# Weighing stage in the program of the expert-activation stage, with the first group prepared in freed buffers

## The chip, the cores and the metric

One core of one Trainium2 chip. The metric is the device time of one execution in microseconds; before the change three runs gave 3397.03, 3400.71 and 3400.64, median 3400.64.

## The reference

A transformer layer over 1024 tokens of width 1024. After the attention part, which the change doesn't touch, comes PEER: every token has 8 heads, each picks 16 of 16,384 single-neuron experts by product keys, and

```python
hid = jnp.einsum('td,tkd->tk', xx, u[ee])          # 128 picks a token
act = jax.nn.gelu(hid, approximate=False) * gg     # gg: softmax share of a pick
out = jnp.einsum('tk,tkd->td', act, v[ee])
```

## The kernel before

Tokens are cut into 8 blocks of 128. Blocks 0 and 1 (`GB = 2`, "first" tokens) are done by gathering the picked rows of `u` and `v`; blocks 2 to 7 (`TD = 768` tokens) densely over all experts, with a gate table that is zero where an expert isn't picked. All matmuls run as three passes of a high and a low fp32r part: high x high, high x low, low x high. A high part is a copy on ScalarE, a low part a subtraction on POOL (GpSimd).

`hidden` (L774) is the **expert-activation stage**: 8 blocks x 16 slots, one slot for each of 128 key rows j. A slot loads `u_raw` on the SyncE queue, rounds it (`u_hi`, ScalarE L918; `u_lo`, POOL L968), runs 48 matmuls of 384 columns (L1299), takes Gelu of them into `hid` (L943) and stores it to `hid_d`. From block 2 on a slot also makes the gate table of 8 tokens: one-hot factors on VectorE (L1017), scaling on ScalarE (L924), 8 matmuls (L1312), a copy to `stage` (L951) that SyncE stores to `gate_d` in quarters of half a block (64 tokens). Beside it, POOL gathers one row of `u` for each first token and pick (L977) and VectorE takes the dot product with `x_first` (L1228) into `pick_act`: `LAG = (8, 16)` slots after the start for the two blocks, and the last 8 and 16 picks in the last block into the freed score table (L987, L1235). Then Gelu and share.

`weigh` (L1788) is the **weighing stage**, in a program block of its own: the one before has to end on all engines first. It sums activation x gate x v over 32 groups of 4 key rows. A group has two halves of 2 rows. For a half SyncE loads `v_raw` (1 MB, one buffer) and `act_in` (768 KB, one buffer a half) and once a group `gate_in` (1.5 MB, one buffer); VectorE multiplies gates in (L1940), ScalarE rounds (`v_hi` L1897, `act_hi` L1899), POOL makes `v_lo` (L1924) and `act_lo` (L1929). TensorE then runs, for each of 6 token blocks, 24 matmuls of 512 columns (L2006; 144 a group) into one of two PSUM accumulators `part`, and VectorE adds that to `acc` (L1945). For the first tokens POOL gathers a row of `v` for each pick k (`found`, 4 buffers; two DMAs, L1915) and VectorE adds it to `first_sum` (L1953): 128 picks, four a group in all 32 groups.

The order on each engine is written out by hand, and every engine works strictly in its order. What matters here: a buffer's next load waits on SyncE until its low part is made; a gather waits on POOL until its buffer's last pick is summed, and the low parts stand behind it; on VectorE the product with the gates of the group after next stands between the adds:

```python
add(g, 4)
if left >= 2:
    gates(g + 2, 0)
add(g, 5)
add_pick(g, 3)
```

TensorE's wait for a group's halves stands at token block 0, ahead of row 0 and of row 2.

Of the kernel before, what the change touches and what calls it, by code (L numbers as in the profile page):

```python
# [396 lines left out]

class Shared:

    def __init__(self, nc, c, sem):  # L400
        self.banks = c.enter_context(nc.psum_tensor("banks", [P, 8, HALF], F))

        with ExitStack() as first:
            def sb(name, shape, dt=F):
                return first.enter_context(nc.sbuf_tensor(name, shape, dt))
# [23 lines left out]
        self.pick = sb("pick", [P, PEER_HEADS, K], U32)
        self.share = sb("share", [P, PEER_HEADS, K])  # L430
        self.col_t = sb("col_t", [P, P])
        self.score = sb("score", [P, 2 * PEER_HEADS, NK])
        self.found = sb("found", [P, GB, D])
        self.stage = sb("stage", [P, 2, NK, 64])
        self.top = sb("top", [P, PEER_HEADS, 2, K])
        self.top_ix = sb("top_ix", [P, PEER_HEADS, 2, K], U32)
        self.top_ixf = sb("top_ixf", [P, PEER_HEADS, 2, K])
        self.pick_part = sb("pick_part", [P, 2, PEER_HEADS, K], U32)
        self.expert = sb("expert", [P, 2, PEER_HEADS, K])
        self.row_t = sb("row_t", [P, P])  # L440
        self.g_t = sb("g_t", [P, P])
        self.pick_u = sb("pick_u", [P, GB, PICKS], U32)
        self.pick_share = sb("pick_share", [P, GB, PICKS])
# [6 lines left out]
        self.sc_out = sem("sc_out")  # L450


def route(nc, block, sem, m, a_hi, a_lo, x_first, ident, x_d, w_out_d, norm_g_d, wq_d, keysT_d, h_d, uT_d, score_d):
# [10 lines left out]
    with ExitStack() as c:  # L464
        def sb(name, shape, dt=F):
            return c.enter_context(nc.sbuf_tensor(name, shape, dt))

        w_raw, w_hi, w_lo, h, xs, gain, keysT = m.w_raw, m.w_hi, m.w_lo, m.h, m.xs, m.gain, m.keysT
        qT = xs[:, 0].rearrange("p (s n) -> p s n", s=2)
        rest = xs[:, 1, 0:HALF].rearrange("p (b n) -> p b n", b=4)  # L470
        sc = xs[:, 1, HALF:D].rearrange("p (b n) -> p b n", b=4)
        top, top_ix = m.key_top, m.key_ix
        tick = sb("tick3", [P, 4])
        ss = sb("ss3", [P, TB])
        rstd = sb("rstd3", [P, TB])
        neg_half = sb("neg_half3", [P, 1])
        pr_ps = m.banks[:, 0:4]
        tr_ps = m.banks[:, 4:6].rearrange("p b (c n) -> p (b c) n", c=C // 2)
        sc_ps = m.banks[:, 6:8].rearrange("p s (b n) -> p s b n", b=4)

        x_in = sem("x_in3")
        small_in = sem("small_in3")

        first_in = [sem(f"first_in3{n}") for n in range(4)]
        first_hi = sem("first_hi3")
        first_lo = [sem(f"first_lo3{n}") for n in range(4)]
        w_in = sem("w_in3")
        w_hi_ok = sem("w_hi_ok3")
        w_lo_ok = sem("w_lo_ok3")
        u_in, u_hi_ok, u_lo_ok = m.u_in, m.u_hi_ok, m.u_lo_ok  # L490
        const_ok = sem("const_ok3")
        pr_ok = sem("pr_ok3")
        added = sem("h_added")
        h_out = sem("h_out")
        ss_ok = sem("ss_ok3")
        var_ok = sem("var_ok3")
        rstd_ok = sem("rstd_ok3")
        xs_ok = sem("xs_ok3")
        tr_ok = sem("tr_ok3")
        hi_ok = sem("hi_ok3")  # L500
        lo_ok = sem("lo_ok3")
        q_ok = m.q_ok
        sc_ok = sem("sc_ok")
        first_ok = sem("first_ok3")
        rest_ok = sem("rest_ok3")
        second_ok = sem("second_ok3")
        top_ok = m.top_ok
        sc_sb = sem("sc_sb")
        sc_out = m.sc_out
        SCORED = 4 * ITEMS  # L510

        @block.sync
        def _(sp):
            def load_w(g):
                src = w_out_d[:, g * HALF:(g + 1) * HALF] if g < 2 else wq_d[:, (g - 2) * HALF:(g - 1) * HALF]
                if g == 1:
                    for part in range(4):
                        sp.wait_ge(first_lo[part], 1)
                else:
                    sp.wait_ge(w_lo_ok, 4 * (g - 1))  # L520
                sp.dma_start(w_raw[:, :, :], src.rearrange("(c p) n -> p c n", p=P)).then_inc(w_in, 16)

            def load_u(j):
                sp.dma_start(m.u_raw[:, :, :], uT_d[j]).then_inc(u_in, 16)

            for part in range(4):
                s = slice(2 * part, 2 * part + 2)
                sp.dma_start(w_raw[:, s], w_out_d[2 * part * P:(2 * part + 2) * P, 0:HALF]
                             .rearrange("(c p) n -> p c n", p=P)).then_inc(first_in[part], 16)
            sp.dma_start(h[:, :, :], x_d.rearrange("(b p) n -> p b n", p=P)).then_inc(x_in, 16)  # L530
            sp.dma_start(gain[:, :], norm_g_d.unsqueeze(0).to_broadcast([P, D])).then_inc(small_in, 16)
            load_w(1)
            sp.dma_start(keysT[:, :, :], keysT_d.rearrange("k d n -> d k n")).then_inc(small_in, 16)
            load_w(2)
            for tb in range(TB):
                sp.wait_ge(added, TB + tb + 1)
                sp.dma_start(h_d[tb * P:(tb + 1) * P, :], h[:, tb]).then_inc(h_out, 16)
            load_w(3)
            for n in range(SCORED):
                if n == ITEMS:  # L540
                    load_w(4)
                if n == 2 * ITEMS:
                    load_w(5)
                if n == 3 * ITEMS:
                    sp.wait_ge(xs_ok, TB)
                    load_u(0)
                if n == SCORED - 2:
                    sp.wait_ge(u_lo_ok, 1)
                    load_u(1)
                key = n // 2  # L550
                if n % 2:
                    sp.wait_ge(sc_sb, key + 1)
                    sp.dma_start(score_d[:, :, key * NK:(key + 1) * NK].rearrange("b t n -> t b n"),
                                 sc[:, :, :]).then_inc(sc_out, 16)

        @block.gpsimd
        def _(pool):
            pool.memset(neg_half[:, :], -0.5).then_inc(const_ok, 1)
            pool.wait_ge(const_ok, 1)

            def split_low(g):
                for part in range(4):
                    s = slice(2 * part, 2 * part + 2)
                    pool.wait_ge(w_hi_ok, g)
                    pool.tensor_tensor(w_lo[:, g % 2, s], w_raw[:, s], w_hi[:, g % 2, s].bitcast(F),
                                       ALU.subtract).then_inc(w_lo_ok, 1)

            for part in (0, 2):
                s = slice(2 * part, 2 * part + 2)
                pool.wait_ge(first_hi, part + 1)  # L570
                pool.tensor_tensor(w_lo[:, 0, s], w_raw[:, s], w_hi[:, 0, s].bitcast(F),
                                   ALU.subtract).then_inc(first_lo[part], 1)
            split_low(1)
            for tb in range(TB):
                pool.wait_ge(var_ok, tb + 1)
                pool.tensor_tensor(rstd[:, tb:tb + 1], ss[:, tb:tb + 1], neg_half[:, 0:1],
                                   ALU.pow).then_inc(rstd_ok, 1)
                if tb == 2:
                    split_low(2)
# [1552 lines left out]
```

## Time and profile before

| | us |
|---|---|
| median of 3 runs | 3400.64 |
| profiled execution | 3400.2 |
| its span, first to last instruction | 3398.4 |
| TensorE busy | 3167.1 |
| VectorE, POOL, ScalarE busy | 2187.0, 1693.5, 1222.5 |
| first matmul of `hidden` / of `weigh` | 1009.2 / 2317.4 |
| last matmul chain of `weigh` ends | 3381.5 |

The profile is one execution. Times are from the span's start. "PEclk" is the granted clock of TensorE as a share of 2.4 GHz, "<-" names what ended an idle time. A busy share over the whole span says little here; the rows below are therefore read by stretch.

### The profile page before, as it was taken

The page shows a single profiled execution, that of the slowest core. Times are in us where ns is not written, and L with a number is a line of the kernel's source. Part 1 is how long each engine was busy: PE and PEld are TensorE (multiplying, and loading weights), DVE is VectorE, ACT ScalarE, POOL GpSimd, SP SyncE. Part 2 cuts the span into 40 slices and gives each one's busy share as a digit, 9 for nine tenths or more (in the row PEclk, how much of TensorE's full clock was granted, in tenths as well). Part 3 has the DMA queues.
Part 4 walks back from the last instruction along what each step waited for, and adds up shares of the span by engine and source line. Part 5 has one row for each costly group of instructions (what it writes and reads, how often), then busy time and mean ns, then how long its engine had stood idle before and what let it go on. Part 6 is the DMA issues. An engine that isn't in the chain of part 4 may idle for free. (4 is left out here: it accounts for less than half of the span.)

```text
span 3398.4 us, 44061 instructions
## 1 busy us (share of the span) xinstructions
PE 3167.1 (93%) x17090; PEld 2861.5 (84%) x17090; DVE 2187.0 (64%) x3550; ACT 1222.5 (36%) x1895; POOL 1693.5 (50%) x847
## 2 busy tenths in 40 slices
PE   7989688988999999999999999985999999999998
PEld 5777578877889999999999999984888888888886
DVE  2510578824456778788988888763766666666665
ACT  3211347722112225656565656651122211222110
POOL 2411010012103565555556555765877878778683
PEclk9999799999999999999999999997999999999999
DMA  3242651141213676767677767898878778787784
GB/s 137 87 167 75 154 112 41 35 161 62 72 41 132 201 238 203 248 236 249 235 247 238 251 234 237 314 329 319 298 284 308 278 280 308 270 306 283 274 295 162
DMA packets 253394, 713.78 MB, mean 210 GB/s; under 512 B 21680, under 2 KB 79920, under 8 KB 246576
## 3 DMA queue, kind: packets, MB, share of 16 engines
q1 hardware_dynamic: 179504, 443.13, 38.2%
q0 software_dynamic: 73728, 268.47, 22.9%
q8 instruction: 104, 1.70, 0.2%
q14 instruction: 58, 0.48, 0.0%
HBM read 577.31 MB, written 134.22 MB: 209 GB/s over the span
## 5 line engine op out<-in xcount | busy, mean ns | idle before, releaser
L1228 DVE SCALAR_TENSOR_TENSOR found<-found,x_first 128x1024 f32<-128x1024 f32 x232 | 393.9, 1708 | 238.4 <-DMA found<-in_u,pick_u 237.5
L968 POOL TENSOR_TENSOR u_lo<-u_raw,u_hi 128x1024 fp32r<-128x1024 f32 x127 | 353.8, 2786 | 367.0 <-ACT u_hi L918 366.6
L1299 PE MATMUL banks<-side_hi,u_hi 128*128 128x384 f32 x2048 | 528.5, 339 | 0.0
L2006 PE MATMUL part<-v_hi,act_hi 128*128 128x512 f32 x1536 | 475.9, 391 | 48.9 <-POOL act_lo L1929 48.0
L1299 PE MATMUL banks<-side_hi,u_lo 128*128 128x384 f32 x2048 | 520.3, 334 | 0.0
L1299 PE MATMUL banks<-side_lo,u_hi 128*128 128x384 f32 x2048 | 520.2, 334 | 0.0
L2006 PE MATMUL part<-v_lo,act_hi 128*128 128x512 f32 x1536 | 474.8, 390 | 0.0
L2006 PE MATMUL part<-v_hi,act_lo 128*128 128x512 f32 x1536 | 474.6, 390 | 0.0
L977 POOL DMA_INDIRECT found<-in_u,pick_u x232 | 334.7, 1443 | 188.9 <-DVE found L1228 148.5
L1945 DVE TENSOR_TENSOR acc<-acc,part 128x1024 f32<-128x1024 f32 x192 | 234.1, 1219 | 297.6 <-PE part L2006 297.4
L1897 ACT ACTIVATE v_hi<-v_raw 128x2048 fp32r<-128x2048 f32 x64 | 122.8, 1919 | 808.9 <-DMA v_raw<-in_v 623.9
L1924 POOL TENSOR_TENSOR v_lo<-v_raw,v_hi 128x2048 fp32r<-128x2048 f32 x64 | 295.8, 4621 | 190.4 <-ACT v_hi L1897 189.8
L2006 PEld LDWEIGHTS part<-v_hi,act_hi 128*128 128x128 f32 x1536 | 289.5, 189 | 110.6 <-issue 49.0
L1299 PEld LDWEIGHTS banks<-side_hi,u_lo 128*128 128x128 f32 x2048 | 370.2, 188 | 0.0
L1299 PEld LDWEIGHTS banks<-side_lo,u_hi 128*128 128x128 f32 x2048 | 370.1, 188 | 0.0
L1299 PEld LDWEIGHTS banks<-side_hi,u_hi 128*128 128x128 f32 x2048 | 364.7, 188 | 0.0
L2006 PEld LDWEIGHTS part<-v_lo,act_hi 128*128 128x128 f32 x1536 | 289.8, 189 | 60.4
L2006 PEld LDWEIGHTS part<-v_hi,act_lo 128*128 128x128 f32 x1536 | 289.5, 189 | 60.2
L1915 POOL DMA_INDIRECT found<-in_v,pick_v x256 | 292.0, 1141 | 62.6 <-issue 53.1
L1953 DVE SCALAR_TENSOR_TENSOR first_sum<-found,pick_act,first_sum 128x1024 f32<-128x1024 f32 x256 | 316.5, 1281 | 0.0
L924 ACT ACTIVATE col_gate<-col_gate,g_t 128x128 f32<-128x128 f32 x768 | 234.8, 391 | 96.8 <-DVE col_gate L1017 96.6
L943 ACT ACTIVATE hid<-banks 128x768 f32<-128x768 f32 x128 | 103.5, 809 | 377.2 <-PE banks L1299 377.1
(217 smaller groups left out, 5201.4 us busy)
## 6 DMA issues: line engine op xcount, KB each, us to landing
u_raw<-in_uT SPq DMA_DIRECT2D x128, 512.0 KB, 3.5
v_raw<-in_v SPq DMA_DIRECT2D x64, 1024.0 KB, 5.2
hid_d<-hid SPq DMA_DIRECT2D x128, 384.0 KB, 5.1
gate_d<-stage SPq DMA_DIRECT2D x48, 1024.0 KB, 8.3
act_in<-hid_d SPq DMA_DIRECT2D x64, 768.0 KB, 6.9
gate_in<-gate_d SPq DMA_DIRECT2D x32, 1536.0 KB, 14.3
w_raw<-in_w_in SPq DMA_DIRECT2D x6, 2048.0 KB, 8.2
k_hi<-k_hi_d SPq DMA_DIRECT2D x32, 256.0 KB, 7.8
```

The lines of the kernel that those rows point to most:

```text
L924: last = act.activation(col_gate[:, s % 2, i], col_gate[:, s % 2, i], ACT.Copy, scale=g_t[:, t:t + 1])
L943: act.activation(hid[:, s % 2].rearrange("p (h n) -> p h n", h=2), hid_ps[:, s % 2, :, 0:W], ACT.Gelu).then_inc(hid_ok, 1)
L968: pool.tensor_tensor(u_lo[s % 2][:, :, :], u_raw[:, :, :], u_hi[s % 2][:, :, :].bitcast(F), ALU.subtract).then_inc(u_lo_ok, 1)
L977: pool.indirect_dma_start(found[:, g], None, u_d, bass.IndirectOffsetOnAxis(ap=pick_u[:, g, n:n + 1], axis=0))\
L1228: dve.scalar_tensor_tensor(out=found[:, g], in0=found[:, g], scalar=1.0, in1=x_first[:, g], op0=ALU.mult, op1=ALU.mult, accum_out=pick_act ...
L1299: mm = pe.matmul(hid_ps[:, s % 2, half, 0:W], w[s % 2][:, ch], x[:, ch, GB * P + half * W:GB * P + (half + 1) * W], start=n == 0, stop=n = ...
L1897: act.activation(v_hi[:, s, half(x)], v_raw[:, :, :], ACT.Copy).then_inc(v_hi_ok, 1)
L1915: pool.indirect_dma_start(found[:, b, k % PICK], None, v_d.rearrange("j i d -> (j i) d"), bass.IndirectOffsetOnAxis(ap=pick_v[:, b, k:k + ...
L1924: pool.tensor_tensor(v_lo[:, s, half(x)], v_raw[:, :, :], v_hi[:, s, half(x)].bitcast(F), ALU.subtract).then_inc(v_lo_ok, 1)
L1945: dve.tensor_tensor(acc[:, n], acc[:, n], part[:, n % BANKS], ALU.add).then_inc(added, 1)
L1953: dve.scalar_tensor_tensor(out=first_sum[:, b], in0=found[:, b, n], scalar=pick_act[:, b, bass.ds(k, 1)], in1=first_sum[:, b], op0=ALU.mul ...
L2006: last = pe.matmul(part[:, n % BANKS, cols], a[:, s, j, rows], v[:, s, j, cols], start=j == 0 and m == 0, stop=j == J - 1 and m == 2)
```

## The change

`weigh` moves into the block of `route` and `hidden`. Its buffers are laid out by hand over those of `hidden` (`Shared`), so that each can be written as soon as what lies there is used up; `v_hi` and `v_lo` take the place of the transposed tokens `side_hi` and `side_lo` (now `x_hi`, `x_lo`). Waits stand where the block's end stood.

In `hidden`: `LAG` is (6, 11) and the late picks (7, 12), all of them in slots 0 to 12 of the last block; the ranking of blocks 0 and 1 takes 11 slots instead of 15. After slot 12 of the last block SyncE loads the activations of group 0 (`act_first`, `act_in[1]`), after slot 13 its gates for 704 of the 768 tokens and its four rows of v (`v_raw`, `found4[1]`). VectorE multiplies, ScalarE rounds, VectorE and POOL share the low parts. In `weigh`: the gates of the last 64 tokens are taken from `stage` in SBUF; token block 5, which has them, waits for them. `acc` is loaded in six pieces. Group 0 has no V picks; groups 1 and 2 have six each (`group_of_six`), then four. The diff, cut to its core:

```diff
+        self.lag = (6, 11)
+        self.late = (7, 12)
     # hidden, sync
+        def load_first_rows():
+            for n in range(2):
+                sp.wait_ge(hid_out[n], 16 * blocks)
+            sp.wait_ge(stage_out[0], 16 * PARTS * (blocks - GB))
+            sp.wait_ge(stage_out[1], 16 * PARTS * (blocks - GB - 1))
+            for x, rows in ((0, m.act_first), (1, m.act_in[1])):
+                sp.dma_start(rows[:, :, :], hid_d[COLS * x:COLS * x + COLS].rearrange("j i t -> i j t"))\
+                    .then_inc(m.a_in[x], 16)
+        def load_first():
+            sp.dma_start(m.gate_in[:, 0:EARLY_Q], gate_d[0:EARLY_Q, :, 0:2 * COLS].rearrange("q i j t -> i q j t"))\
+                .then_inc(m.g_in, 16)
+            sp.dma_start(m.v_raw[:, :, :], v_d[0:COLS].rearrange("j i d -> i j d")).then_inc(m.v_in, 16)
             for g in range(GB):
+                sp.wait_ge(late_dotted[g], LATE[g])
+            sp.dma_start(m.found4[1][:, :, :], v_d[COLS:2 * COLS].rearrange("j i d -> i j d"))\
+                .then_inc(m.v_in, 16)
     # hidden, scalar, last slot
+                if last and s == SLOTS - 1:
+                    high_first()
...
+                if last and s == SLOTS - 1:
+                    high_first_v()
     # weigh, sync
+        for n in range(DENSE):
+            if n == 2:
+                sp.wait_ge(m.gate_mm, DENSE * 16)
+            sp.dma_start(acc[:, n], h_d[(GB + n) * P:(GB + n + 1) * P]).then_inc(acc_in[n >= BANKS], 16)
+        sp.wait_ge(m.gate_ok, DENSE * 16)
+        for n in range(4):
+            store_last(n)
+        load_v(1, 0)
+        for s in range(2):
+            sp.wait_ge(m.hid_out[s], 16 * ALL_STEPS // 2)
+        load_act(1, 1)
+        load_act(1, 0)
+        load_gates(1)
+        load_v(1, 1)
+        sp.dma_start(found[3][:, :, :], h_d[0:GB * P].rearrange("(b p) d -> p b d", p=P)).then_inc(h_in, 16)
+        sp.wait_ge(m.last_out[1], 48)
+        load_act(2, 0)
+        load_gates(2)
+        load_v(2, 0)
+        load_act(2, 1)
+        load_v(2, 1)
+        load_act(3, 0)
+        load_gates(3)
     # weigh, gpsimd
+        for g in range(1, GROUPS):
...
+                pool.tensor_tensor(v_lo[:, cols], v_raw[:, :, :], v_hi[:, cols].bitcast(F),
+                                   ALU.subtract).then_inc(v_lo_ok, 1)
+                if g >= 4 or q == 7:
+                    gather(2 * q - 1)
+                pool.wait_ge(a_hi_ok, q + HALVES + 1)
+                pool.tensor_tensor(a_lo[s][x], act_in[x][:, :, :], a_hi[s][x].bitcast(F),
+                                   ALU.subtract).then_inc(a_lo_ok, 1)
+                if g >= 3:
+                    gather(2 * q)
+                else:
+                    for k in range(3):
+                        gather(6 * (g - 1) + 3 * x + k)
     # weigh, vector
+        def last_gates(x):
+            rows = act_in[1] if x else m.act_first
+            dve.wait_ge(m.gate_ok, DENSE * 16)
+            a = rows[:, :, EARLY_T:]
+            dve.tensor_tensor(a, a, m.stage[:, 1, COLS * x:COLS * x + COLS], ALU.mult).then_inc(gated, 1)
+        def group_of_six(g):
+            def next_pick(n):
+                k = 6 * (g - 1) + n
+                pick(k, k % PICK, k // PICK)
+            add(g, 0)
+            next_pick(0)
+            add(g, 1)
+            gates(g + 1, 1)
+            add(g, 2)
+            next_pick(1)
+            next_pick(2)
+            add(g, 3)
+            next_pick(3)
+            add(g, 4)
+            gates(g + 2, 0)
+            next_pick(4)
+            add(g, 5)
+            next_pick(5)
+        add(0, 0)
+        for x in range(HALVES):
+            last_gates(x)
+        add(0, 1)
+        dve.wait_ge(m.pick_ok, 1)
+        dve.tensor_tensor(pick_act[:, :, :], pick_act[:, :, :], m.pick_share[:, :, :], ALU.mult).then_inc(seeded, 1)
+        add(0, 2)
+        gates(1, 0)
+        add(0, 3)
+        gates(1, 1)
+        add(0, 4)
+        dve.wait_ge(h_in, 16)
+        dve.tensor_copy(first_sum[:, :, :], found[3][:, :, :]).then_inc(seeded, 1)
+        add(0, 5)
+        gates(2, 0)
```

## Rows read from the trace of the kernel before

**Rows 1.** Stretches: length, engine busy times (instructions), clock, DMA share, GB/s
```profile
2113.00:2281.00 168.00, 165.52 (x1050) 164.61 (x1048) 122.45 (x146) 99.88 (x176) 118.19 (x72) 1.00 0.88 309
2281.30:2317.40 36.10, 0.03 (x1) 0.06 (x1) 7.83 (x11) 8.34 (x6) 9.01 (x4) 0.57 0.92 346
2317.40:2369.50 52.10, 39.33 (x156) 31.37 (x157) 22.75 (x14) 7.21 (x5) 36.84 (x18) 0.86 0.84 311
2500.00:2800.00 300.00, 300.00 (x1325) 248.48 (x1324) 194.46 (x149) 63.62 (x38) 232.44 (x109) 1.00 0.80 288
```
**Rows 2.** Waits of TensorE from 2281 on: total us, times, longest
```profile
PE part L2006 <- POOL act_lo L1929: 48.0, 3, 36.2
```
**Rows 3.** Chain that ended last, from the seam on: start, us, what
```profile
2310.32 1.77 DVE act_in L1940
...
2312.12 1.49 ACT act_hi L1899
...
2313.68 3.56 POOL act_lo L1929
...
2369.53 1011.96 PE part L2006 x4452
```
**Rows 4.** Timeline of TensorE at the seam: start, us, what, idle before
```profile
2280.83 0.39 PE L1312 MATMUL banks<-col_gate,row_hot 128*128 128x128 f32 x2
...
2330.10 1.19 PE L2006 MATMUL part<-v_hi,act_hi 128*128 128x512 f32 x2 [8.39 <-POOL act_lo L1929]
```
**Rows 5.** Timeline of VectorE in groups 0 and 2
```profile
2334.97 1.22 DVE L1945 TENSOR_TENSOR acc<-acc,part 128x1024 f32<-128x1024 f32 x1 [4.96 <-PE part L2006]
...
2401.12 2.48 DVE L1940 TENSOR_TENSOR act_in<-act_in,gate_in 128x1536 f32<-128x1536 f32 x1 [3.02 <-DMA gate_in<-gate_d]
...
2404.65 2.47 DVE L1953 SCALAR_TENSOR_TENSOR first_sum<-found,pick_act,first_sum 128x1024 f32<-128x1024 f32 x2
```
**Rows 6.** DMA issues of the whole run: count, KB each, median us to landing
```profile
v_raw<-in_v SPq DMA_DIRECT2D x64, 1024.0 KB, 5.2
hid_d<-hid SPq DMA_DIRECT2D x128, 384.0 KB, 5.1
gate_d<-stage SPq DMA_DIRECT2D x48, 1024.0 KB, 8.3
act_in<-hid_d SPq DMA_DIRECT2D x64, 768.0 KB, 6.9
gate_in<-gate_d SPq DMA_DIRECT2D x32, 1536.0 KB, 14.3
...
acc<-h_d SPq DMA_DIRECT2D x1, 3072.0 KB, 17.2
```
**Rows 7.** Two short stretches of the seam, columns as in the first group
```profile
2297.80:2317.30 19.50, 0.00 (x0) 0.00 (x0) 3.52 (x2) 5.95 (x4) 8.04 (x2) 0.50 0.96 343
2317.30:2321.80 4.50, 4.34 (x12) 3.21 (x12) 0.00 (x0) 0.72 (x1) 4.10 (x3) 0.67 1.02 410
```
**Rows 8.** Timeline of POOL in groups 0 and 1
```profile
2317.37 0.96 POOL L1915 DMA_INDIRECT found<-in_v,pick_v  x1
2318.63 0.94 POOL L1915 DMA_INDIRECT found<-in_v,pick_v  x1 [0.30 <-issue]
...
2344.72 4.61 POOL L1924 TENSOR_TENSOR v_lo<-v_raw,v_hi 128x2048 fp32r<-128x2048 f32 x1 [12.42 <-ACT v_hi L1897]
```
**Rows 9.** Timelines of SyncE's queue and of ScalarE in group 2
```profile
2381.77 0.37 SPq L1847 DMA_DIRECT2D v_raw<-in_v  x1
...
2389.82 0.37 SPq L1859 DMA_DIRECT2D gate_in<-gate_d  x1
...
2386.64 1.92 ACT L1897 ACTIVATE v_hi<-v_raw 128x2048 fp32r<-128x2048 f32 x1 [8.36 <-DMA v_raw<-in_v]
```
**Rows 10.** Timelines of POOL and TensorE around the last slot of `hidden`
```profile
2266.07 2.39 POOL L968 TENSOR_TENSOR u_lo<-u_raw,u_hi 128x1024 fp32r<-128x1024 f32 x1
...
2270.87 0.59 PE L1299 MATMUL banks<-side_hi,u_hi 128*128 128x384 f32 x2
```

More of the change, by code:

```diff
@@ L463, in route @@
     KEYS = 2 * PEER_HEADS
[L464 to L524, printed above, removed]
@@ new lines, in route @@
+    x_in = sem("x_in3")
+    small_in = sem("small_in3")
+    first_in = [sem(f"first_in3{n}") for n in range(4)]
+    first_lo = [sem("first_lo_pool"), sem("first_lo_dve")]
+    w_in = sem("w_in3")
+    w_hi_ok = sem("w_hi_ok3")
+    w_lo_ok = sem("w_lo_ok3")
+    u_in, u_hi_ok, u_lo_ok = m.u_in, m.u_hi_ok, m.u_lo_ok
+    const_ok = sem("const_ok3")
+    pr_ok = sem("pr_ok3")
+    added = sem("h_added")
+    h_out = sem("h_out")
+    ss_ok = sem("ss_ok3")
+    var_ok = sem("var_ok3")
+    rstd_ok = sem("rstd_ok3")
@@ L556, in _ @@
[L556 to L579, printed above, removed]
-            for g in range(3, G):
-                split_low(g)
-            pool.wait_ge(u_hi_ok, 1)
-            pool.tensor_tensor(m.u_lo[0][:, :, :], m.u_raw[:, :, :], m.u_hi[0][:, :, :].bitcast(F), ALU.subtract).then_inc(u_lo_ok, 1)
@@ new lines, in hidden @@
+    LAG = m.lag
+    LATE = m.late
+    COLS = 2
+    EARLY_Q = TD // STAGE - 1
+    EARLY_T = EARLY_Q * STAGE
+    u_raw, u_hi, u_lo = m.u_raw, m.u_hi, m.u_lo
+    hid, stage, row_hot, col_gate, score, found = m.hid, m.stage, m.row_hot, m.col_gate, m.score, m.found
+    cand = score.rearrange("p (h x) (y b) -> p h (x y) b", x=2, b=K)
+    top, top_ix, top_ixf, pick_part, expert = m.top, m.top_ix, m.top_ixf, m.pick_part, m.expert
+    best, pick, share = m.best, m.pick, m.share
+    pick_partf = top.rearrange("p h c k -> p c h k")
@@ new lines, in _, with low_u, gather, gather_late @@
+    @block.gpsimd
+    def _(pool):
+        def low_u(j, s):
+            pool.wait_ge(u_hi_ok, j + 1)
+            pool.tensor_tensor(u_lo[s % 2][:, :, :], u_raw[:, :, :], u_hi[s % 2][:, :, :].bitcast(F),
+                               ALU.subtract).then_inc(u_lo_ok, 1)
+        def gather(g, n):
+            if n:
+                pool.wait_ge(dotted[g], n)
+            else:
+                pool.wait_ge(kept, g + 1)
+            pool.indirect_dma_start(found[:, g], None, u_d,
+                                    bass.IndirectOffsetOnAxis(ap=pick_u[:, g, n:n + 1], axis=0))\
+                .then_inc(found_in[g], 16)
+        def gather_late(g, n):
+            if n:
+                pool.wait_ge(late_dotted[g], n)
+            else:
+                pool.wait_ge(looked, LOOKS * blocks)
+            k = PICKS - LATE[g] + n
+            pool.indirect_dma_start(late(g), None, u_d,
+                                    bass.IndirectOffsetOnAxis(ap=pick_u[:, g, k:k + 1], axis=0))\
+                .then_inc(late_in[g], 16)
+        def body(tb, phase, last):
+            for s in range(SLOTS):
+                j = tb * SLOTS + s
+                if not (last and s == SLOTS - 1):
+                    low_u(j + 1, s + 1)
+                for g in range(GB):
+                    if LAG[g] <= j < LAG[g] + PICKS - LATE[g]:
+                        gather(g, j - LAG[g])
+                if last:
+                    for g, n in late_picks(s):
+                        gather_late(g, n)
+        for tb in range(blocks):
+            body(tb, tb, tb == blocks - 1)
+        pool.wait_ge(m.a_hi_ok, 1)
+        pool.tensor_tensor(m.a_lo[0][0][:, :, 0:EARLY_T], m.act_first[:, :, 0:EARLY_T],
+                           m.a_hi[0][0][:, :, 0:EARLY_T].bitcast(F), ALU.subtract).then_inc(m.a_lo_ok, 1)
+        pool.wait_ge(m.v_hi_ok, 3)
+        pool.tensor_tensor(x_lo[:, 2], m.found4[1][:, 0], x_hi[:, 2].bitcast(F),
+                           ALU.subtract).then_inc(m.v_lo_ok, 1)
@@ new lines, in _, with turn, body @@
+    @block.tensor
+    def _(pe):
+        def turn(tb):
+            pe.wait_ge(looked, LOOKS * (tb + 1))
+            for n, src in enumerate((expert[:, 0], expert[:, 1], share[:, :, :])):
+                last = pe.transpose(turn_ps[:, n], src.rearrange("p h k -> p (h k)"), ident[:, :])
+            last.then_inc(turned, 1)
+        def body(tb, phase, last):
+            for s in range(SLOTS):
+                j = tb * SLOTS + s
+                pe.wait_ge(u_lo_ok, j + 1)
+                if phase == 0 and s < 2:
+                    pe.wait_ge(m.q_ok, 2 * SLOTS)
+                if not (phase == 0 and s < 2):
+                    pe.wait_ge(hid_ok, j - 1)
+                n = 0
+                for ch in range(C):
+                    for w, x in ((u_hi, x_hi), (u_hi, x_lo), (u_lo, x_hi)):
+                        for half in range(2):
+                            mm = pe.matmul(hid_ps[:, s % 2, half, 0:W], w[s % 2][:, ch],
+                                           x[:, ch, GB * P + half * W:GB * P + (half + 1) * W],
+                                           start=n == 0, stop=n == 3 * C - 1)
+                        n += 1
+                mm.then_inc(hid_mm, 1)
+                if s == 15 and phase and not last:
+                    turn(tb + 1)
+                if phase < GB:
+                    continue
+                if not (phase == GB and s == 0):
+                    pe.wait_ge(gate_ok, j - NO_GATES)
+                pe.wait_ge(col_ok, j - NO_GATES + 1)
+                for t in range(TOK):
+                    mm = pe.matmul(gate_ps[:, t], row_hot[:, s % 2, t], col_gate[:, s % 2, t],
+                                   start=True, stop=True)
+                mm.then_inc(gate_mm, 1)
+        for tb in range(GB + 1):
+            body(tb, tb, False)
+        for tb in range(GB + 1, blocks - 1):
+            body(tb, GB + 1, False)
+        body(blocks - 1, GB + 1, True)
@@ new lines, in weigh @@
+    EARLY_Q = TD // STAGE - 1
+    EARLY_T = EARLY_Q * STAGE
+    acc, v_raw, act_in, gate_in, a_hi, a_lo = m.acc, m.v_raw, m.act_in, m.gate_in, m.a_hi, m.a_lo
+    found = m.found4
+    part = m.banks[:, 0:4].rearrange("p (s h) n -> p s (h n)", h=2)
+    first_sum = m.banks[:, 4:8].rearrange("p (b h) n -> p b (h n)", h=2)
+    h_in = sem("h_in")
+    v_in = m.v_in
+    a_in = m.a_in
+    g_in = m.g_in
+    gated = m.gated
+    v_hi_ok = m.v_hi_ok
+    v_lo_ok = m.v_lo_ok
+    a_hi_ok = m.a_hi_ok
@@ new lines, in _, with high @@
+    @block.scalar
+    def _(act):
+        def high(g, s):
+            for x in range(HALVES):
+                act.wait_ge(v_in, 16 * (HALVES * g + x + 1))
+                if isinstance(g, int) and g == 1:
+                    act.wait_ge(m.last_out[0], 16)
+                    act.wait_ge(m.last_out[1], 48)
+                else:
+                    act.wait_ge(part_ok, DENSE * (g - 1))
+                act.activation(v_hi[:, J * s + COLS * x:J * s + COLS * x + COLS], v_raw[:, :, :],
+                               ACT.Copy).then_inc(v_hi_ok, 1)
+                act.wait_ge(gated, HALVES * (g + 1) + x + 1)
+                act.activation(a_hi[s][x], act_in[x][:, :, :], ACT.Copy).then_inc(a_hi_ok, 1)
+        for x, rows in ((0, m.act_first), (1, act_in[1])):
+            act.wait_ge(gated, HALVES + x + 1)
+            act.activation(a_hi[0][x][:, :, EARLY_T:], rows[:, :, EARLY_T:], ACT.Copy).then_inc(a_hi_ok, 1)
+        high(1, 1)
+        with act.Fori(1, TURNS) as p:
+            high(2 * p, 0)
+            high(2 * p + 1, 1)
```

1748 lines of the change are left out of this document (895 added, 853 removed), and 3 rows, old and new, of the table EXPERT_SIGNALS.

## The prediction

> **What bounds the kernel now.** I read the busy time by stretch first. TensorE is busy for 165.5 of the last 168 us of the expert-activation stage, for 300 of 300 us in the middle of the weighing stage, and at full clock in both; between them lie 36.1 us without a matmul and 52.1 us in which it is busy for 39.3 at a clock of 0.86 [rows 1]. So the program is TensorE-bound except at this one seam, and only the seam can pay. The waits say what ends it: 48.0 us in three waits for `act_lo` on POOL, the longest 36.2 [rows 2]. The chain of waits shows what is behind that: the gate load, the gate product on VectorE, `act_hi` on ScalarE, `act_lo` on POOL, and from 2369.53 on nothing but TensorE, 4452 matmuls in 1011.96 us, 0.227 us each [rows 3]. 4608 matmuls of the stage at 0.227 us are 1045 us; from 2281.2, the end of the last gate matmul [rows 4], to 3381.5 [rows 3] are 1100.3 us. **55 us** is all that there is to win at the seam: some 49 us of idling and 6 us of cold clock. One cold restart is seen at 2330.10: VectorE can add that token block at 2334.97 [rows 4, 5], 4.9 us for 12 matmuls that take 2.7 warm, so 2.2 us each time.
>
> **What is costed at nothing.** Everything ahead of the last block is the same work in the same order, with the dots six or eleven slots after the start instead of eight or sixteen. TensorE is full there, and the faster ranking of the two first blocks runs on VectorE beside it. The added two-input VectorE and POOL instructions of the handover (two 128x1408 gate products, some 1.6 us each by the 1.77 of a 128x1536 one [rows 3], the four `v_lo` parts, two `act_lo` parts) lie behind the last two slots' matmuls or delay group 0 by a few us only, and group 0 has slack as shown next. If that cover is gone they cost what they take, about 4 us.
>
> **The sum.** I follow one point through both kernels: the moment POOL's `act_lo` of a group's second half is ready, since TensorE can't pass expert row 2 of token block 0 before. Before, this is 2369.5 for group 1 (R1) [rows 3]; later groups find it ready, so TensorE passes it for group 3 at 2369.5 + 2.2 + 2 x 32.7 = 2437.1 (144 matmuls x 0.227 = 32.7 us a group).
>
> Group 0 starts at about 2282 instead of 2317, as its operands are ready. But group 1 needs loads that the single SyncE queue gives out behind others: the last hid row (384 KB), acc (3072), four stage stores (4096), v (1024), two act_in (1536), gate_in (1536) [rows 6]: 11,648 KB, 11.9 MB. The rate is 343 GB/s in one stretch of the seam and 410 in another [rows 7]; I take 385, nearer the full stretch: 31 us, and 1.5 for the start and end, so the gates land at 2313.5 (2310 at 410, 2317 at 343). The Trainium skill, "DMA: Bandwidth & Descriptors", section "Where 436 GB/s comes from", holds that HBM limits one core to about 358 GB/s, which would make it 2315.8 and the whole sum 2.3 us longer; the 410 of the row is above that, and the row decides. Then gate product 1.8, `act_hi` 1.5, `act_lo` 3.6 [rows 3]: 2320.4. Then POOL issues gathers 0, 1 and 2 (six DMAs, one each 1.26 us [rows 8], 7.6; I add 1 as some take over 2 us), v_lo 4.6 [rows 8], act_lo 3.6: **R1 = 2337**, 32.5 us earlier than before. TensorE's own losses until then (token block 5 waits for `add(0, 3)`, which stands behind the gate wait on VectorE, to about 2316; then the wait for R1) end by R1 and are no term.
>
> Now the added waits. Groups 1 and 2 have six picks each; POOL works in order, and a gather waits until its buffer's last pick is summed. Queued behind these waits are `v_lo` and `act_lo`, and TensorE waits for those.
> (a) gather(5) waits for pick 1, which VectorE takes after `add(1, 2)`. From R1: block 0 cold 4.9, two blocks 10.9, add 1.2 [rows 5], pick 2.5 [rows 5], second half of the gather 1.2: R1 + 20.7. v_lo 4.6 and act_lo 3.6 of group 2's first half: R1 + 29.0.
> (b) Only then can SyncE load act_in and gate_in for group 3. Such a gate load takes 11.3 us from issue (2389.8) to the product (2401.1) [rows 5, 9] and 14.3 in the median [rows 6]; I take 12, nearer the one in this stretch, and 0.5 for the issue: R1 + 41.5. `group_of_six(1)` has `gates(3, 0)` ahead of pick 4, and gather(8), in POOL's queue ahead of the second half of group 2, needs pick 4. Gates 1.8, first half of the pick 1.3, gather 2.5, v_lo 4.6, act_lo 3.6, gaps 0.2: **R2 = R1 + 55.5**. Without waits it would be 34.9: TensorE stands for 20.6 us.
> (c) Group 3: gather(11) waits for pick 7 in the same place, so first half `v_lo` done at R2 + 25.4; only then is the second half of v loaded (4.9 us from 2381.8 to 2386.6) and rounded (1.9) [rows 9]: 32.2; v_lo 36.9, gather(13) 39.4, act_lo: **R3 = R2 + 43.1**, 8.2 us over 34.9.
> Group 4 has four gathers, none behind a gate wait of its own: about R3 + 30, no stall.
>
> R3 = 2337 + 55.5 + 43.1 = 2435.6, and a cold restart of 2.2: 2437.8 against 2437.1 before. The 32.5 us won by R1 are given back: **+0.7 us**. I add 1 us for the first loads competing with the last slots (below): span 3398.4 + 1.7 = 3400.1, with the 1.8 us that the profiled time has around its span 3401.9, so **3402 us**. The profiled execution (3400.2) and the median (3400.64) are the same to 0.5 us.
>
> As a check, the price of the clock. Before there are three restarts after a wait, after the change four (block 5 of group 0, R1, R2, R3). The Trainium skill, "TensorE: Matmul & The Clock Gate", section "HAM oscillation — how this bites in real kernels", says that several short gaps each pay the fall of the clock again, which speaks against cutting one long gap into pieces; the trace agrees, with a clock of 0.50 ahead of and 0.67 after the first restart [rows 7]. The sum has these restarts in it with the 2.2 us of the row.
>
> **Rivals.** *Waits that don't chain (faster).* For it: POOL has idle time at the seam, and a landed gate load costs nothing. If gates(3, 0) are there when VectorE reaches them, gather(8) doesn't wait; R2 = R1 + 29.0 + 7.6 + 8.2 + 0.2 = R1 + 45, 10.5 us less: 3391. If neither gather waits, TensorE bounds all from R1 and the 28.8 us of (b) and (c) and two restarts fall away: 3369. Against it: the act_in buffer of the first half is single, so the load can't precede R1 + 29. Chances 0.20 and 0.08.
> *The seam's traffic delays the last slots and R1 (slower).* Place: slots 12 to 15 of the last block, where 1536 KB of act_in, 1408 KB of gates and 2048 KB of v are now loaded beside the gathers, less about five late gathers (512 KB each). The stretch already moves 309 GB/s [rows 1]; net 2.4 MB more in 31 us makes it some 390, just under 410. TensorE has little cover: the last `u_lo` ends at 2268.5, its use begins at 2270.9 [rows 10]. It decides from a delay of 2.4 us of that load on, or a queue at 343 GB/s after. Price: up to 4 us there, 3.5 us in R1, 2.4 in (b) with the median landing, and 1 to 2 us if gathers run at 2 us: +12: 3414. Chance 0.30.
> *The early first group does nothing.* Group 0 could be early and R1 not: that is bounded by 2369.5 for R1, the sum then 3434. Nothing in the rows holds R1 that late, as its bytes are the same and begin 16 us sooner; 0.02, within the slower case.
>
> **How the numbers follow.** Forecast 0.40 (3402, its own range 3394 to 3407.5); faster 0.28; slower 0.32. Faster by over 0.2% means below 3393.8, slower above 3407.4, about what a measurement of this kernel can tell from no change. The range reaches from 3380, which leaves out the last faster case, to 3419, which leaves out most of the third rival and the tail of the second.
>
> **What would show it.** In the profile after: first matmul of the weighing stage within some 3 us of 2281; the waits of TensorE in groups 0 to 3 in four pieces, near 6, 10, 21 and 8 us, the 21 us one ended by `act_lo`; POOL idle ahead of gather(5), gather(8) and gather(11), released by the picks on VectorE; VectorE idle some 12 us ahead of gates(3, 0) with the gate load as releaser. TensorE without waits from group 4 on, and 0.227 us a matmul. The forecast is wrong if R1 is off by over 6 us, if the 21 us wait isn't there, or if the stage before the seam changes its length by over 4 us.

## The result, and the profile after

The changed kernel takes 3441.97 us (median of four runs), the kernel before 3400.22 beside it: ratio 1.0128, 95% interval 1.011 to 1.0146. It is 42 us slower; 3402 was forecast, and 3441.97 lies outside the range of 3380 to 3419, on the slower side. One of the executions behind the numbers below, 3447.38 us in before_pad32, shows a granted clock of 0.906 where all others show 0.968 to 0.975; it is a slow one and is left out.

The profile's span grew from 3398.4 to 3439.8 us. The engines' busy times, page after:

```profile
PE 3217.4 (94%) x17090; PEld 2873.1 (84%) x17090; DVE 2154.5 (63%) x3556; ACT 1224.4 (36%) x1899; POOL 1680.5 (49%) x847
```

TensorE runs the same 17,090 matmuls, but is busy 50.3 us longer (3167.1 before). That is the first oddity: the change was to move idle time, and here is more busy time. The stretches of the kernel after, which answer [rows 1, 7] (length, then PE, PEld, DVE, ACT, POOL busy with counts, granted clock, DMA share, GB/s):

```profile
2290.40:2347.20 56.80, 39.60 (x157) 31.20 (x157) 23.09 (x20) 12.24 (x12) 26.70 (x14) 0.86 0.91 338
2347.20:2405.00 57.80, 35.77 (x144) 28.36 (x144) 26.66 (x21) 6.59 (x4) 27.25 (x16) 0.80 0.63 217
2405.00:2448.60 43.60, 35.90 (x145) 28.43 (x145) 18.62 (x15) 6.59 (x4) 25.51 (x14) 0.89 0.67 231
2500.00:2800.00 300.00, 300.00 (x1288) 240.99 (x1287) 183.51 (x144) 60.20 (x36) 227.22 (x108) 1.00 0.78 282
```

The first three are the seam, cut at the forecast's points R1, R2, R3. The last row is the finding: in the same 300 us, at full clock and without a gap, TensorE gets through 1288 matmuls instead of 1325 [rows 1]. Each takes 300/1288 = 0.233 us, not 0.226. The timeline of TensorE says the same line by line (start, us; each row is two matmuls, so starts lie two matmuls apart), first before, then after:

```profile
2699.95 0.62 PE L2006 MATMUL part<-v_hi,act_hi 128*128 128x512 f32 x2
2700.41 0.62 PE L2006 MATMUL part<-v_lo,act_hi 128*128 128x512 f32 x2
```
```profile
2700.28 0.63 PE L2203 MATMUL banks<-side_hi,act_hi 128*128 128x512 f32 x2
2700.75 0.63 PE L2203 MATMUL banks<-side_lo,act_hi 128*128 128x512 f32 x2
```

0.46 us a pair against 0.47. Over all matmuls that start between 2500 and 3200 us the mean distance from one start to the next is 226.67 ns before and 233.33 ns after. Read the starts: the duration of a row, 0.62 and 0.63, hides it, as matmuls overlap.

The waits of TensorE after 2280, which answer [rows 2], and the chain that ended last at the seam, which answers [rows 3]:

```profile
PE banks L2203 <- POOL act_lo L2078: 40.8, 3, 22.0
PE banks L2227 <- DVE side_lo L1392: 5.8, 1, 5.8
```
```profile
2347.19 16.20 PE banks L2203 x60
...
2366.10 0.94 POOL found L2059
2367.34 0.94 POOL found L2059
2368.31 4.63 POOL side_lo L2073
2372.94 3.47 POOL act_lo L2078
2377.14 14.43 DMA gate_in<-gate_d
...
2396.13 0.94 POOL found L2059
2397.09 4.51 POOL side_lo L2073
2401.60 3.38 POOL act_lo L2078
2405.02 16.30 PE banks L2203 x60
...
2431.08 5.08 DMA v_raw<-in_v
2436.18 1.93 ACT side_hi L2030
2438.18 4.56 POOL side_lo L2073
...
2448.60 974.25 PE banks L2203 x4164
```

This is the chain that was forecast, link for link: block 0, pick 1, `gather(5)`, the low parts of group 2's first half, the gate load, pick 4 and `gather(8)`, the low parts of the second half, and once more with the late load of v. The last row again has the finding: 974.25 us for 4164 matmuls, 0.234 each.

Where the 41.4 us of span are: `hidden` begins at 1017.7 instead of 1009.2 (+8.5), and lasts 1272.7 instead of 1272.0 us (+0.7). From the last gate matmul, 2290.4, to the end of the span are 1149.4 us instead of 1117.2 (+32.2). So most of it is spread over stretches in which TensorE waits for nothing, and 8.5 us lie ahead of anything that the change was said to touch.

### The profile page after: what moved, and what is told of

The parts are those of the page before. It is cut to its first block, busy times and chain, and to the rows that moved or that the text cites. A ratio compares the mean times of both kernels' runs of the same rounds, so it can differ in the third digit from the quotient of the medians.

```text
span 3439.8 us, 44129 instructions
## 1 busy us (share of the span) xinstructions
PE 3217.4 (94%) x17090; PEld 2873.1 (84%) x17090; DVE 2154.5 (63%) x3556; ACT 1224.4 (36%) x1899; POOL 1680.5 (49%) x847
## 4 chain that ended last, share of the span: by engine, by line
PE 60%; DMA 8%; DVE 5%; POOL 4%; issue 2%; ACT 1%; DVEq 0%; SPq 0%; POOLq 0%; ACTq 0%
PE banks L2203 29%; PE banks L1417 19%; DMA found<-in_u,pick_u 6%; PE banks L808 5%; PE banks L1430 3%; PE banks L787 2%; DVE found L1338 2%; POOL u_lo L1071 1%; DVE col_gate L1126 1%; PE banks L816 1%; POOL side_lo L2073 1%; POOL found L1080 1%; DVE row_hot L1126 1%; DMA v_raw<-in_v 1%; ACT col_gate L1006 1%
## 5 line engine op out<-in xcount | busy, mean ns | idle before, releaser
L2203 PE MATMUL banks<-side_hi,act_hi 128*128 128x512 f32 x1488 | 470.6, 397 | 40.8 <-POOL act_lo L2078 40.8
L2107 DVE TENSOR_TENSOR acc<-acc,banks 128x1024 f32<-128x1024 f32 x192 | 234.6, 1222 | 404.5 <-PE banks L2203 390.0
L2203 PE MATMUL banks<-side_lo,act_hi 128*128 128x512 f32 x1488 | 470.1, 397 | 0.0
L2203 PE MATMUL banks<-side_hi,act_lo 128*128 128x512 f32 x1488 | 469.4, 396 | 0.0
L2030 ACT ACTIVATE side_hi<-v_raw 128x2048 fp32r<-128x2048 f32 x62 | 119.1, 1921 | 834.3 <-PE banks L2203 426.4
L2073 POOL TENSOR_TENSOR side_lo<-v_raw,side_hi 128x2048 fp32r<-128x2048 f32 x62 | 286.5, 4621 | 181.6 <-ACT side_hi L2030 181.0
L2203 PEld LDWEIGHTS banks<-side_hi,act_hi 128*128 128x128 f32 x1488 | 280.1, 189 | 110.6 <-POOL act_lo L2078 30.6
L2203 PEld LDWEIGHTS banks<-side_lo,act_hi 128*128 128x128 f32 x1488 | 280.6, 189 | 68.9
L2203 PEld LDWEIGHTS banks<-side_hi,act_lo 128*128 128x128 f32 x1488 | 280.4, 188 | 68.9
L2115 DVE SCALAR_TENSOR_TENSOR banks<-found,pick_act,banks 128x1024 f32<-128x1024 f32 x192 | 237.5, 1283 | 0.0
## 6 DMA issues: line engine op xcount, KB each, us to landing
gate_in<-gate_d SPq DMA_DIRECT2D x31, 1536.0 KB, 14.9
```

What stands on the lines that cost most here:

```text
L2030: act.activation(v_hi[:, J * s + COLS * x:J * s + COLS * x + COLS], v_raw[:, :, :], ACT.Copy).then_inc(v_hi_ok, 1)
L2073: pool.tensor_tensor(v_lo[:, cols], v_raw[:, :, :], v_hi[:, cols].bitcast(F), ALU.subtract).then_inc(v_lo_ok, 1)
L2107: dve.tensor_tensor(acc[:, n], acc[:, n], part[:, n % BANKS], ALU.add).then_inc(added, 1)
L2115: dve.scalar_tensor_tensor(out=first_sum[:, b], in0=found[n][:, b], scalar=pick_act[:, b, bass.ds(k, 1)], in1=first_sum[:, b], op0=ALU.mul ...
L2203: last = pe.matmul(part[:, n % BANKS, cols], a, v[:, cols], start=j == 0 and k == 0, stop=j == J - 1 and k == 2)
```

## The experiments

In the stretch from 2500 to 2800 us the matmuls are the same in shape and clock, and no other engine holds them up. What differs is **where their operands lie in SBUF**. Read from the program, in bytes of a partition: before, `v_hi` lies at 51,328 and `act_hi` at 141,440, `side_hi` at 18,560 and `w_hi` of the routing stage at 130,176. Each of the two differences is a multiple of 256. After, `side_hi` is still at 18,560, but six small tiles, 192 bytes in all and 224 with each rounded up to 32, stand ahead of the tiles that the stages now share, and these begin at 93,536: the difference between the two operands of a matmul is 224 more than a multiple of 256 in `weigh` and in the routing stage.

Theory A: the addresses cost the time. Rival B: the addresses do nothing, and it is the place of the stage (one program block, a PSUM tile of eight banks, another code address).

**Experiment 1, after_pad32.** 32 bytes put the shared tiles at 93,568, a multiple of 256 from `side_hi`. Nothing else changes.

```diff
         self.tick = small("tick", [P, 6])
+        small("pad", [P, 8])
```

> The kernel after the change with one unused tile of 32 bytes a partition ahead of all tiles that route, hidden and weigh share; every such tile moves from an address that is 32 over a multiple of 64 bytes to a multiple of 64. Nothing else changes. Theory A (the address of a matmul operand costs time): matmuls of 512 columns in route and weigh go from 233.4 ns apart back to 226.7 ns, 6.7 ns x (4608 + 1152) = 38.6 us less, about 3403 us. Rival B (the place of the v parts in the tokens' old tiles, or the one common program, slows TensorE): 3442 us, 233.4 ns as after the change. In both the waits of TensorE in groups 1 to 3 stay at about 11, 22 and 8 us.

Measured: 3401.8 us against 3397.61 before, ratio 1.0017 (1.0007 to 1.0026), span 3399.1. The middle of `weigh` (stretch, columns as above) and its end of chain:

```profile
2500.00:2800.00 300.00, 300.00 (x1325) 248.47 (x1325) 196.96 (x148) 63.66 (x38) 230.79 (x110) 1.00 0.80 290
```
```profile
2435.21 946.99 PE banks L2204 x4164
```

1325 matmuls again, and 27.3 us less for the same 4164. A pad of 32 bytes gives back 40 us by the two medians, and 38 when each kernel is compared with the one before that ran beside it. So B falls, and an address is the cause; whether it is an operand's own address or the distance between two is asked next. What is left of the change is 0.17%, with an interval that reaches from 0.07 to 0.26%: a little slower, if anything.

**Experiment 2, before_pad32.** Is it the absolute address (an operand that isn't on a multiple of 64)? All tiles of `weigh` in the kernel before are moved by 32 bytes.

```diff
+        sb("pad", [P, 8])
         acc = sb("acc", [P, DENSE, D])
```

> The kernel before with one unused tile of 32 bytes a partition ahead of all tiles of the weighing stage, which moves them all to 32 over a multiple of 64 bytes. Theory A: 4608 matmuls at 233.4 ns instead of 226.7, 31 us more, about 3431 us; route keeps 226.7 ns. Rival B: no change, 3400 us.

Measured: 3401.47 us (median of nine runs), ratio 1.0011 (1.0001 to 1.0021).

```profile
2500.00:2800.00 300.00, 300.00 (x1325) 248.43 (x1324) 211.69 (x150) 63.40 (x38) 235.08 (x109) 1.00 0.80 288
```

No slower matmul: theory A as I had put it, that an operand off a multiple of 64 costs, **fell**. Both operands had moved together. What was left was their difference.

**Experiments 3 and 4, before_weights32 and before_moving32.** In the kernel before, one operand alone is moved: the weights `act_hi`, `act_lo`, or the moving `v_hi`, `v_lo`; a second pad behind it keeps what follows in step. Experiment 3, then 4:

```diff
+        sb("pad", [P, 8])
         a_hi = sb("act_hi", [P, 2, J, TD], R)
         a_lo = sb("act_lo", [P, 2, J, TD], R)
+        sb("pad_after", [P, 8])
```
```diff
+        sb("pad", [P, 8])
         v_hi = sb("v_hi", [P, 2, J, D], R)
         v_lo = sb("v_lo", [P, 2, J, D], R)
+        sb("pad_after", [P, 8])
```

> The kernel before with act_hi and act_lo alone (the stationary operand of the weighing stage, 128 columns loaded as weights) moved by 32 bytes; v_hi and v_lo stay. If the stationary operand's address costs: 233.4 ns apart, 3431 us. If only the moving operand's does: 226.7 ns, 3400 us.

> The kernel before with v_hi and v_lo alone (the moving operand of 512 columns) moved by 32 bytes; act_hi and act_lo stay. If the moving operand's address costs: 233.4 ns apart, 3431 us. If only the stationary operand's does: 226.7 ns, 3400 us. The out-projection of route after the change (moving operand moved, stationary not) was slow, so I expect 233.4 here too.

Measured (one run each): 3427.59 and 3430.77 us. The same 300 us, experiment 3 and then 4:

```profile
2500.00:2800.00 300.00, 300.00 (x1288) 241.50 (x1287) 181.76 (x143) 60.41 (x36) 227.11 (x108) 1.00 0.78 280
```
```profile
2500.00:2800.00 300.00, 300.00 (x1287) 241.53 (x1286) 184.45 (x144) 60.36 (x36) 226.22 (x108) 1.00 0.78 283
```

Either way the matmuls take the 0.233 us of the kernel after, in the kernel before, with its block structure and its PSUM tiles untouched. It is the difference between the two addresses that counts. (Inside the tiles of `weigh` every slice starts a multiple of 512 bytes on, so these runs can't tell whether the partner of a moving operand is its own weights or the next matmul's, loaded meanwhile.)

**Experiment 5, after_both32.** The reverse in the kernel after: `side_hi` is moved by 32, and with it, by 64, the shared tiles. Routing and `weigh` have a multiple of 256 again; the projections of the first stage (L377), which were in step, lose it.

```diff
+            sb("pad", [P, 8])
             side_hi = sb("side_hi", [P, C, T], R)
             side_lo = sb("side_lo", [P, C, T], R)
+            sb("pad_after", [P, 8])
             ident = sb("ident", [P, P])
```

> The kernel after the change with unused tiles of 32 bytes ahead of side_hi and behind side_lo: side_hi and side_lo now lie at 32 over a multiple of 64 bytes, as the tiles shared by route, hidden and weigh do already. Theory (only the difference of the two operands' addresses counts, modulo 64): weighing and route at 226.7 ns, and project, where the weights of the projection stay on multiples of 64, slows from 226.7 to 233.4 ns, 1152 matmuls x 6.7 ns = 7.7 us: 3402 + 8 = 3410 us. Rival (an operand off a multiple of 64 costs by itself): 233.4 ns in the weighing stage, 3450 us.

Measured (one run): 3414.47 us. `weigh` is at 1325 in the stretch:

```profile
2500.00:2800.00 300.00, 300.00 (x1325) 248.39 (x1324) 197.62 (x149) 62.19 (x38) 240.29 (x115) 1.00 0.82 295
```

The projection has become slower. Groups by line (busy us, mean ns of one), first the kernel before, then experiment 5:

```profile
L377 PE MATMUL pr_ps<-w_hi,side_hi 128*128 128x512 f32 x256 | 100.8, 394 | 0.2 <-POOL w_lo L186 0.2
```
```profile
L377 PE MATMUL pr_ps<-w_hi,side_hi 128*128 128x512 f32 x256 | 102.2, 399 | 0.3 <-POOL w_lo L186 0.3
```

The cost has moved to another stage, as the difference says: the 1152 matmuls of the projection start 233.3 ns apart where they follow each other without a gap, against 226.7 in experiment 1, and those of the routing stage are back at 227. `hidden` begins at 1018.1, 10.7 us later than in experiment 1; 1152 matmuls at 6.7 ns are 7.7 of these. In the groups by line I find 1.3 us more in the attention's `o_ps` matmuls (283 ns each instead of 277) and 1.2 in a wait for `prob`. The kernel after has both too, but so has experiment 6 below (286 ns), in which no tile of the attention lies elsewhere than before; so this part varies from run to run and isn't the pads'.

**Experiments 6 and 7, before_weights64 and before_weights128.** How far must one operand move? As experiment 3 without the second pad, by 64 and by 128 bytes (`[P, 32]` in place of `[P, 16]`).

```diff
+        sb("pad", [P, 16])
         a_hi = sb("act_hi", [P, 2, J, TD], R)
```

> The kernel before with act_hi, act_lo and found4 moved by 64 bytes; v_hi and v_lo stay. If operands only have to agree modulo 64: 226.7 ns apart, 3400 us. If they have to agree modulo 128 or more: 233.4 ns or slower, 3431 us or more.

> The kernel before with act_hi, act_lo and found4 moved by 128 bytes; v_hi and v_lo stay. A shift by 32 and one by 64 bytes cost 30 us. If the two operands have to agree modulo 128: 226.7 ns apart, 3398 us. If modulo 256 (in the fast kernels with 32 bytes of padding they differ by 256 modulo 512): 233.4 ns, 3430 us.

Measured (one run each): 3432.92 and 3428.97 us.

```profile
2500.00:2800.00 300.00, 300.00 (x1287) 241.70 (x1287) 182.08 (x143) 60.34 (x36) 224.59 (x109) 1.00 0.78 280
```
```profile
2500.00:2800.00 300.00, 300.00 (x1287) 241.35 (x1286) 181.35 (x143) 60.39 (x36) 226.65 (x107) 1.00 0.77 280
```

Differences of 32, 64, 128 and 224 above a multiple of 256 all cost the same 3% (233.33 ns from start to start in each of these runs), those of 0 cost nothing (226.67 ns). Why it is so, and whether other differences in between would be fast, stays open.

**Experiments 8 and 9** turn to the seam itself, with the pad of experiment 1 in. Does the chain of gathers and gate loads set the time there, as the sum has it? **pick_first** puts pick 4 ahead of the gates that it stood behind:

```diff
             add(g, 4)
-            gates(g + 2, 0)
             next_pick(4)
+            gates(g + 2, 0)
             add(g, 5)
```

> The kernel after_pad32 with one line moved: in a group of six VectorE takes pick 4 before the gates of the group after next, so that gather(8) doesn't wait for a gate load. Theory: from R1 to R2 45 us instead of 57.7, R2 to R3 unchanged at 43.8, about 3389 us. Rival (the second half of v, loaded late, is what ends the wait): R2 unchanged, 3402 us.

Measured: 3393.26 us, ratio 0.9985 (0.9973 to 0.9996), span 3391.7. Waits of TensorE, and its timeline where the wait for group 2's second half ends:

```profile
PE banks L2204 <- POOL act_lo L2079: 26.3, 3, 9.2
```
```profile
2384.49 1.22 PE L2204 MATMUL banks<-side_hi,act_hi 128*128 128x512 f32 x2 [9.23 <-POOL act_lo L2079]
```

In experiment 1 the same line of the waits reads 42.6, 3, 22.4. R1 is 2340.97 in this run, so R2 - R1 is 43.5 us instead of 57.7, and R3 - R2 (2428.73) is 44.2 instead of 43.8: the long wait fell from 22 to 9 us, and nothing else moved. `hidden` ended some 7 us later in this run than in experiment 1 (2285 and 2277), which takes back half of it: by spans it is 7.4 us, by the medians 8.5, by the points 13.8; the 3389 that I expected was missed by 4. The seam's term is shown; the net gain is known less well.

**four_picks** drops the groups of six. Each group from the first on takes four picks, of the group before it, and the four that are left over stand in group 31:

```diff
-                if g >= 4 or q == 7:
-                    gather(2 * q - 1)
+                if g >= 2 or x:
+                    gather(2 * (q - 2) - 1)
...
-                if g >= 3:
-                    gather(2 * q)
-                else:
-                    for k in range(3):
-                        gather(6 * (g - 1) + 3 * x + k)
+                gather(2 * (q - 2))
+        for k in range(4, 0, -1):
+            gather(PICKS - 1 - k)
...
-            pick(PICK * g + n, n, g)
+            pick(PICK * (g - 1) + n, n, g - 1)
...
-        group_of_six(1)
-        group_of_six(2)
+        group(1, 2)
+        group(2, 2)
...
-        group(GROUPS - 1, 0)
+        k = PICKS - 2 * PICK
+        for n, picks in enumerate((2, 1, 1, 1, 2, 1)):
+            add(GROUPS - 1, n)
+            for _ in range(picks):
+                pick(k, k % PICK, k // PICK)
+                k += 1
```

> The kernel after_pad32 without the groups of six picks: groups 1 to 31 have four each, in the order of the kernel before with one group's delay, and the last four picks are spread over group 31. The extra gathers no longer stand ahead of the low parts. Theory (the gathers that wait for picks hold back v_lo and act_lo): the point R1 5 us earlier, 22.8 us less from R1 to R2 and 11.1 from R2 to R3, one cold restart less: about 3361 us, and TensorE without a wait from R1 on. Rival (the loads of the seam, not the picks, set when the halves of groups 2 and 3 are ready): the waits at R2 and R3 stay above 15 and 5 us, 3395 us.

Measured: **3367.72 us**, ratio 0.9913 (0.9892 to 0.9934) to the kernel before. Waits, and TensorE's last piece of the chain:

```profile
PE banks L2186 <- POOL act_lo L2079: 7.8, 1, 7.8
PE banks L2210 <- DVE side_lo L1393: 4.5, 1, 4.5
PE banks L2210 <- DVE acc L2106: 1.9, 1, 1.9
```
```profile
2334.87 1005.61 PE banks L2186 x4428
```

Behind R1 there is no wait at all. R1 itself is 53.7 us behind the last gate matmul here (2281.2), against 56.3 in experiment 1: only 2.5 us earlier, as one gather still stands between the two low parts in POOL's queue. That and a `hidden` that ended 4 us later than in experiment 1 are why 3361 was missed by 7. This is the version that beats both kernels.

## Why the prediction was right and wrong

**The sum at the seam held.** The last gate matmul ends at 2290.4 after instead of 2281.2, so the points are compared from there.

| | forecast | after | experiment 1 |
|---|---|---|---|
| S, last gate matmul | 2281.2 | 2290.4 | 2277.4 |
| R1 - S | 55.8 | 56.8 | 56.3 |
| R2 - R1 | 55.5 | 57.8 | 57.7 |
| R3 - R2 | 43.1 | 43.6 | 43.8 |
| waits in groups 0 to 3 | 6, 10, 21, 8 | 5.8, 11.1, 22.0, 7.7 | 4.6, 11.9, 22.4, 8.3 |

*Early loads and R1.* The product with group 1's gates (VectorE, kernel after; idle before it in brackets):

```profile
2323.86 1.76 DVE L2093 TENSOR_TENSOR act_in<-act_in,gate_in 128x1536 f32<-128x1536 f32 x1 [6.08 <-DMA gate_in<-gate_d]
```

That is S + 33.5, forecast S + 32.3. So 11.9 MB took about 32 us, and 385 GB/s was slightly high: the profile has 374 over the 31.9 us from S. The 358 of the Trainium skill ("DMA: Bandwidth & Descriptors", section "Where 436 GB/s comes from") gave S + 34.6, which is as near to S + 33.5 as the forecast was; the rate itself was above it here. (At 410 GB/s the gates land at 2311.8 and not at the 2310 of the working; nothing rests on that.) Behind it POOL's `act_lo` took 4.6 us, not 3.6, and the six gathers 7.3, not 8.6, so these two misses cancel.

*(a) gather(5).* POOL, kernel after, first gather(5) and then gather(8):

```profile
2366.10 0.94 POOL L2059 DMA_INDIRECT found<-in_v,pick_v  x1 [8.96 <-DVE banks L2115]
...
2394.89 0.94 POOL L2059 DMA_INDIRECT found<-in_v,pick_v  x1 [13.65 <-DVE banks L2115]
```

The low part behind the first begins at R1 + 21.1 (forecast 20.7). *(b) the gate load.* It was issued at 2377.14, and VectorE began the product 14.5 us later:

```profile
2391.66 1.76 DVE L2093 TENSOR_TENSOR act_in<-act_in,gate_in 128x1536 f32<-128x1536 f32 x1 [15.83 <-DMA gate_in<-gate_d]
```

I had taken 12, nearer the one load of the stretch before than the median of 14.3 [rows 6, 9]. The median was right. The product began at R1 + 44.5 instead of R1 + 41.5, what followed it was 0.7 us shorter, and so R2 - R1 was short by 2.3. *(c)* was right to 0.5 us.

**The step that failed is the first of the working: "What is costed at nothing".** It held everything ahead of the last block to be the same work, and the whole sum took "0.227 us a matmul" from the kernel before for every matmul after. Both kernels do run the same matmuls, but the change moved their operands. That row of cost had no entry:

- routing stage: 1152 matmuls of 512 columns x 6.7 ns = 7.7 us, of the 8.5 by which `hidden` starts later;
- `weigh`: 4608 x 6.7 ns = 30.9 us. In the chain it is 974.25 - 946.99 = 27.3 us from R3 on, for 4164 of them.

Together 38.6 us, against 40.2 between the medians of the changed kernel and experiment 1, and 37.6 with each compared with the kernel before beside it. "TensorE without waits from group 4 on" was right; "0.227 us a matmul" behind it was the wrong half of that sentence, and it was also the line that gave the cause away. Without that cost the sum would still not have been right to the 0.2 us by which experiment 1 (3401.8) meets 3402: beside the kernel before of its own runs (3397.61) it is 4.2 us slower, and the sum had 1.7. That it met the number so closely is luck.

**The rivals.** *Waits that don't chain*: false, all three gathers waited, for the reason given against it; experiment 8 shows that it is the place of pick 4 that makes the long one, and experiment 9 what the rival's last case (3369) would have needed: no group of six. It measured 3367.72; that the two numbers are so close is partly chance, as its start of `hidden` and its R1 aren't those of that case. *The seam's traffic*: true in part, and the length of `hidden` hides it (1272.7 us against 1272.0, with waits elsewhere in it that come and go). Look at slot 14 of the last block, from its first 384-column matmul to that of slot 15, as a stretch before and after:

```profile
2260.80:2270.90 10.10, 10.10 (x67) 10.10 (x66) 8.17 (x11) 6.32 (x11) 8.00 (x5) 1.00 0.73 245
```
```profile
2265.80:2280.00 14.20, 11.71 (x66) 11.42 (x65) 8.80 (x10) 6.25 (x11) 7.12 (x4) 0.88 1.03 386
```
```profile
2265.18 1.23 DVE L1338 SCALAR_TENSOR_TENSOR found<-found,x_first 128x1024 f32<-128x1024 f32 x1 [5.78 <-DMA found<-in_u,pick_u]
...
2276.88 3.41 PE L1430 MATMUL banks<-col_gate,row_hot 128*128 128x128 f32 x16 [2.49 <-ACT col_gate L1006]
```

The slot takes 14.2 us instead of 10.1, at 386 GB/s; the rival had said some 390 and up to 4 us. It doesn't come by `u_lo`, as the rival had it: VectorE waits for gathered rows of `u`, makes the next table late, and TensorE waits 2.5 us for `col_gate` and then runs its 16 gate matmuls in 3.41 us instead of 1.95, as its clock has fallen (0.58 in those 3.4 us). In all six runs of the kernel before, padded or not, the slot takes 10.1 us; in the five of the kernel after 14.2, 10.7, 15.8, 15.3 and 11.5 (after, experiments 1, 5, 8, 9). The sum had 1 us for this. It is also most of why `hidden` ended later in experiment 8 than in experiment 1. That the added loads are the cause is read from these rows; no run took them away.

*The early first group does nothing*: false, R1 is 56.8 us behind S, where it was 88.3 (2369.5 - 2281.2). None of the rivals had a mechanism by which a matmul itself changes, so the range could not hold the time.

## What to carry to other kernels

When a change adds, removes or reorders tiles in SBUF, even small ones, work out for each matmul the addresses of its two operands and keep their difference at a multiple of 256 bytes (shown here for fp32r matmuls of 512 columns with 128x128 weights); then compare the count of matmuls in a full 300 us stretch of each stage with that of the kernel before, ahead of any reading of waits. When a handover is made earlier, follow the in-order queues behind it: a gather that waits for a sum behind a gate load, with the low parts queued behind that gather, gave all 31 us back, and four picks instead of six kept them.

## What the runs showed of the hardware

- The spacing of 512-column fp32r matmuls with a weight load each depends on the difference between the addresses of the weights and the moving tile: 226.7 ns at a multiple of 256 bytes, 233.3 ns at 32, 64, 128 or 224 above one, at full clock with nothing waiting. Moving both tiles by 32 bytes costs nothing.
- 384-column matmuls didn't show it: in `hidden` of the kernel after, `u_hi` stands as far out of step with `side_hi`, and in its first two blocks they start 173.3 ns apart in both kernels (48 of them take 8.33 us); a later slot without a wait takes 10.11 us in both. Whether that is due to their size was not tried. The 128-column matmuls with `keysT` are no test: both of their tiles are shared ones, a multiple of 256 apart in both kernels.
- With the handover's loads beside the gathers the core moved 386 GB/s over 14.2 us in the last block of `hidden` (245 in the same slot before), and VectorE waited 5.78 us for gathered rows; over the five runs of the changed kernel and its variants that slot took 0.6 to 5.7 us more than before.
- A gate load of 1.5 MB took 14.4 us from issue to landing with little beside it (217 GB/s over that stretch), no faster than the median of the whole run (14.3 before, 14.9 after).
